# Output projections: the second weight slab split into two halves that TensorE awaits one by one, with ScalarE's table load moved behind the third slab

## The reference

```python
for i in range(DEPTH):                      # DEPTH = 4
    a = rms_norm(h, mix_norm_pre[i])
    m = (dilated_attention_mixer, short_conv_mixer, conformer_conv_mixer)[i % 3](a, ...)
    h = h + rms_norm(m, mix_norm_post[i])
    f = conv_ffn(rms_norm(h, ffn_norm_pre[i]), ffn_w_in[i], ffn_w_conv[i], ffn_w_out[i])
    h = h + rms_norm(f, ffn_norm_post[i])
```

## Time and profile before

| | |
|---|---|
| time of three runs | 2284.12 us median (2284.03 to 2288.83) |
| the profiled execution | 2280.8 us, span 2278.9 us |
| granted TensorE clock, mean | 0.983 |
| TensorE busy | 2190.1 us, 96% |
| weight loads of TensorE busy | 2004.7 us, 88% |
| VectorE busy | 1516.2 us, 67% |
| ScalarE busy | 1010.2 us, 44% |
| GpSimd busy | 461.5 us, 20% |
| chain of work that ended last | TensorE 85%, VectorE 9%, ScalarE 4% |

### The profile page before, as it was taken

One profiled execution on the slowest core, in us unless ns is written; L12 is line 12 of the kernel. 1 busy time (PEld: TensorE's weight loads), 2 busy tenths in 40 slices (PEclk: granted clock), 3 DMA queues, 4 the chain that ended last, 5 costly groups with the idle time before them and its releaser, 6 DMA issues.

```text
span 2278.9 us, 43583 instructions
## 1 busy us (share of the span) xinstructions
PE 2190.1 (96%) x16355; PEld 2004.7 (88%) x16355; DVE 1516.2 (67%) x2436; ACT 1010.2 (44%) x1355; POOL 461.5 (20%) x492
## 2 busy tenths in 40 slices
PE   6999999999999989999999999999999999989999
PEld 5998779978899868699889987799789999869999
DVE  6874868847688577388578848688465545645553
ACT  4334555534455433455443345555353342444342
POOL 2220005500145140035212200055013200100330
PEclk9999999999999989999999999999999999899999
DMA  5555135555545543245555551355545556103554
GB/s 170 184 184 184 38 127 175 185 192 165 192 163 185 178 130 121 69 162 184 180 167 187 185 190 41 109 177 184 190 153 166 175 175 189 43 1 130 184 187 145
DMA packets 299894, 350.28 MB, mean 154 GB/s; under 512 B 7494, under 2 KB 254940, under 8 KB 299804
## 3 DMA queue, kind: packets, MB, share of 16 engines
q1 hardware_dynamic: 298082, 347.07, 46.0%
q10 hardware_dynamic: 1466, 1.80, 0.2%
q0 software_dynamic: 256, 0.17, 0.0%
HBM read 346.34 MB, written 2.68 MB: 153 GB/s over the span
## 4 chain that ended last, share of the span: by engine, by line
PE 85%; DVE 9%; ACT 4%; issue 1%; DMA 1%; SPq 0%; ACTq 0%; DVEq 0%
PE ps L1980 25%; PE ps L1982 25%; PE ps L1981 24%; DVE w_lo L1461 3%; ACT w_hi L1092 2%; PE ps L2310 2%; PE ps L2281 1%; PE ps L2257 1%; DVE res L1583 1%; PE ps L2268 1%; DVE scaled_out L1577 1%; DVE a_lo L1487 1%; PE ps L930 1%; PE ps L2251 1%; DVE hstat L1520 1%
## 5 line engine op out<-in xcount | busy, mean ns | idle before, releaser
L1461 DVE TENSOR_TENSOR w_lo<-raw,w_hi 128x2048 fp32r<-128x2048 f32 (+2 forms) x328 | 744.4, 2270 | 534.4 <-ACT w_hi L1092 534.4
L1980 PE MATMUL ps<-a_hi,w_hi 128*128 128x256 f32 (+1 forms) x3352 | 953.5, 284 | 15.5 <-DVE a_lo L1487 7.6
L1981 PE MATMUL ps<-a_lo,w_hi 128*128 128x256 f32 (+1 forms) x3352 | 948.3, 283 | 0.0
L1982 PE MATMUL ps<-a_hi,w_lo 128*128 128x256 f32 (+1 forms) x3352 | 948.1, 283 | 0.0
L1092 ACT CAST w_hi<-raw 128x2048 fp32r<-128x2048 f32 (+2 forms) x328 | 613.4, 1871 | 626.7 <-PE ps L1982 603.7
L1980 PEld LDWEIGHTS ps<-a_hi,w_hi 128*128 128x128 f32 x3352 | 635.4, 190 | 20.3 <-DVE w_lo L1461 14.4
L1982 PEld LDWEIGHTS ps<-a_hi,w_lo 128*128 128x128 f32 x3352 | 635.8, 190 | 0.0
L1981 PEld LDWEIGHTS ps<-a_lo,w_hi 128*128 128x128 f32 x3352 | 632.7, 189 | 0.1
L1908 POOL TENSOR_TENSOR hs<-sg,cv 128x256 f32<-128x256 f32 x88 | 65.4, 743 | 734.4 <-DVE cv L1745 734.4
L1915 POOL CAST hid_hi<-hs 128x256 f32 (+3 forms) x132 | 140.2, 1062 | 329.1 <-DVE hs L1791 314.9
L1980 PE MATMUL ps<-w_hi,hid_hi 128*128 128x512 f32 x480 | 190.4, 397 | 10.7 <-DVE w_lo L1461 10.4
(11 more groups left out here) (277 smaller groups left out, 2462.0 us busy)
## 6 DMA issues: line engine op xcount, KB each, us to landing
raw<-in_ffn_w_in_dram SPq DMA_DIRECT2D x88, 1024.0 KB, 5.0
raw<-in_attn_w_qkv_dram SPq DMA_DIRECT2D x72, 1024.0 KB, 4.9
raw<-in_ffn_w_out_dram SPq DMA_DIRECT2D x32, 1024.0 KB, 5.0
raw<-in_ffn_w_gate_dram SPq DMA_DIRECT2D x22, 1024.0 KB, 5.1
raw<-in_ffn_w_up_dram SPq DMA_DIRECT2D x22, 1024.0 KB, 5.2
raw<-in_ffn_w_down_dram SPq DMA_DIRECT2D x16, 896.0 KB, 4.7
raw<-in_ffn_w_out_dram SPq DMA_DIRECT2D x16, 768.0 KB, 4.2
raw<-in_sc_w_in_dram SPq DMA_DIRECT2D x12, 1024.0 KB, 5.1
```

The source lines that it names most:

```text
L1461: dve.tensor_tensor(slab_view(w_lo, ph, j, j % 2), slab_view(raw, ph, j, j % 2), slab_view(w_hi, ph, j, j % 2).bitcast(F32), ALU.subtract) ...
L1980: pe.matmul(o, wh, xh, start=start, stop=False)
L1981: pe.matmul(o, wh, xl, start=False, stop=False)
L1982: return pe.matmul(o, wl, xh, start=False, stop=stop)
```

## The change

In an `out` phase the split of slab 1 is cut into two halves of two k tiles each (1024 values per partition instead of 2048). ScalarE raises `hi_half` after the first half and `hi_ready` after the second; VectorE does the same with `lo_half` and `lo_ready`. TensorE waits for `lo_half` before the first matmul of slab 1 and for `lo_ready` before its third k tile of the first token half. The table load of Sqrt moves from ahead of slab 1 to behind the cast of slab 2. Both new semaphores are raised once in a phase, and the wait's value is the count of output projections so far (`B["post"] + 1`).

```diff
--- before.py
+++ after.py
@@ -421,6 +421,7 @@
 
         raw_landed = [sem(f"raw_landed{j}") for j in range(2)]
         hi_ready, lo_ready, mid_used = sem("hi_ready"), sem("lo_ready"), sem("mid_used")
+        hi_half, lo_half = sem("hi_half"), sem("lo_half")
         tile_done, drained_a, drained_b = sem("tile_done"), sem("drained_a"), sem("drained_b")
         x_landed, ident_landed, const_landed = sem("x_landed"), sem("ident_landed"), sem("const_landed")
         hot_landed = sem("hot_landed")
@@ -1089,7 +1090,11 @@
 
                 act.wait_ge(raw_landed[j % 2], (i * (ph.spb // 2) + (ph.s0 // 2 + j // 2 + 1)) * 16)
                 slot_free(act, ph, i, j)
-                act.copy(slab_view(w_hi, ph, j, j % 2), slab_view(raw, ph, j, j % 2)).then_inc(hi_ready, 1)
+                o, src = slab_view(w_hi, ph, j, j % 2), slab_view(raw, ph, j, j % 2)
+                if ph.kind == "out" and j == 1:
+                    act.copy(o[:, 0:2, :], src[:, 0:2, :]).then_inc(hi_half, 1)
+                    o, src = o[:, 2:, :], src[:, 2:, :]
+                act.copy(o, src).then_inc(hi_ready, 1)
 
             def split_ahead(ph, i, is_last):
                 if not is_last:
@@ -1212,7 +1217,6 @@
 
                 elif ph.kind == "out":
                     q0 = 4 * B["post"]
-                    load_table(act, ACT.Sqrt)
 
                     def square(n):
                         act.wait_ge(tile_done, B["t"] + n + 1)
@@ -1233,6 +1237,8 @@
 
                     for j in range(1, ph.spb):
                         split_hi(ph, 0, j)
+                        if j == 2:
+                            load_table(act, ACT.Sqrt)
                     split_ahead(ph, 0, True)
                     square(0)
                     bias_of_root(0, 1)
@@ -1457,9 +1463,14 @@
 
             def split_lo(ph, i, j):
 
+                o, src, hi = slab_view(w_lo, ph, j, j % 2), slab_view(raw, ph, j, j % 2), slab_view(w_hi, ph, j, j % 2)
+                if ph.kind == "out" and j == 1:
+                    dve.wait_ge(hi_half, ph.base["post"] + 1)
+                    dve.tensor_tensor(o[:, 0:2, :], src[:, 0:2, :], hi[:, 0:2, :].bitcast(F32), ALU.subtract
+                                      ).then_inc(lo_half, 1)
+                    o, src, hi = o[:, 2:, :], src[:, 2:, :], hi[:, 2:, :]
                 dve.wait_ge(hi_ready, i * ph.spb + (ph.s0 + j + 1))
-                dve.tensor_tensor(slab_view(w_lo, ph, j, j % 2), slab_view(raw, ph, j, j % 2),
-                                  slab_view(w_hi, ph, j, j % 2).bitcast(F32), ALU.subtract).then_inc(lo_ready, 1)
+                dve.tensor_tensor(o, src, hi.bitcast(F32), ALU.subtract).then_inc(lo_ready, 1)
 
             def split_ahead(ph, i, is_last):
                 if not is_last:
@@ -2147,12 +2158,17 @@
                     kf = sum(ph.kts[0::2])
                     pe.wait_ge(row_ready, B["tok"])
                     for j in range(ph.spb):
-                        slab_split(ph, 0, j)
+                        if j == 1:
+                            pe.wait_ge(lo_half, B["post"] + 1)
+                        else:
+                            slab_split(ph, 0, j)
                         k0 = sum(ph.kts[j % 2:j:2])
                         wh, wl = wide_view(w_hi[j % 2], ph.kts[j]), wide_view(w_lo[j % 2], ph.kts[j])
                         for t in range(2):
                             n, c = 2 * (j % 2) + t, slice(t * P, (t + 1) * P)
                             for k in range(ph.kts[j]):
+                                if j == 1 and t == 0 and k == 2:
+                                    slab_split(ph, 0, 1)
                                 if j % 2 == 0 and t == 0:
                                     pe.wait_ge(hid_ready, B["hid"] - kf + k0 + k + 1)
                                 mm = mm3(out_chunk(n), hid_hi[:, k0 + k, c], hid_lo[:, k0 + k, c], wh[:, k, :], wl[:, k, :],
```

## The result

The changed kernel takes 2272.0 us in the median of six runs (2267.12 to 2278.49), the kernel before 2287.3 in the median of its six (2284.03 to 2288.83). The ratio is 0.9942 with a 95% interval of 0.9925 to 0.9959, which is 13.3 us of 2287 (9 to 17). The forecast was 2269.3 us in a range of 2263.5 to 2276.0 and a gain of 14.8 us. The profiled execution of the changed kernel took 2267.12 us, span 2265.3 against 2278.9. The ratios leave out one slow execution, 3340.8 us long at a mean clock of 0.596, of the kernel with the conformer's slab 1 split early.

A forecast was written before the change was run, and what follows sets the result against it. TensorE was taken to wait for `w_lo` between slabs 0 and 1 of eight output projections. Attentions 1.3, feed-forwards 6.8, short convolution 0.7 and conformer 6.0 make 14.8 us: 2284.1 becomes 2269.3 us, range 2263.5 to 2276.

The forecast's parts named there:

- The waits and their costs: Border of slabs 0 and 1, eight projections: attention costs 0.65 us each, feed-forward 1.70, short convolution about 0.7, conformer 6.63.
- The table load: ScalarE reaches slab 1's cast 1.40 us sooner in seven projections; behind slab 2's cast the load costs nothing.
- The halves: In slab 1's split, half casts take 1.05 us and half subtractions 1.2; the first half alone decides.
- the halves do nothing: Rival, slab 1's split: the table load does all, 8.4 us gained in sum, 2275.7 us; chance 0.06.
- The conformer: Conformer projection's slab border: the pause's cost falls from 3.89 to 0.6 us and the clock's 2.74 go, 6.0 gained.
- the clock's part: Conformer's slab 1 at half clock after the pause: 2.74 us, all to be gained; rival that it isn't, chance 0.10.
- What was late next: Slabs 2 and 3: no new gap; closest case the conformer's slab 3, ready at 955.1 against a need at 955.6.
- The slower rival: Rival, norm pauses behind projections: the clock falls there instead, 4.9 us slower, 2289 us; chance 0.02.
- The base of the forecast: Median of three runs of the kernel before, 2284.1 us, from which the forecast gain was subtracted.

The follow-up runs named there:

- more halves: The changed kernel with slab 1 also split in halves in the phases that follow a norm: 2265.3 us, ratio 0.9917.
- and the conformer's slab 1 early: The kernel with more halves, its conformer's slab 1 also split during the convolution in front of the projection: ratio 0.9918.

## Why the prediction was right

**The waits and their costs.** Each gap cost what the distances of slabs said and not what the idle column said. With 0.34 us of idle time an attention projection gained 0.61 and 0.67, with 1.43 a feed-forward one gained 1.70. That step carried 8.8 us of the sum, and the kernel without the conformer's part measured 8.7 by stages and 8.2 (5.5 to 10.7) by timing.

**The table load.** Hidden behind slab 2's cast as forecast, with 2.11 us of ScalarE's idle time left at the feed-forward.

**The halves.** A half cast was right at 1.05 us. A half subtraction was right at 1.2 us at attention, short convolution and conformer, and too low at the feed-forward by up to 0.5, where GpSimd shares the time. The forecast had named 0.3 for that. The slack of TensorE covered it. In the changed kernel the halves matter least: with the load moved, the whole slab is in time without them in six projections. Only at the short convolution (0.6 us) and at the conformer do they shorten a pause. The rival "the halves do nothing" came near this but was wrong by size: it expected 8.4 where the table load alone gave 12.3 by stages. 1.0 of the difference is at the feed-forward ones, where it had a subtraction of 2.58 us that takes 2.29 at its new time; 2.9 are at the conformer, 4.3 against its 1.4, since it left slab 1 at half the clock, and slab 1 took 5.67 us there.

**The conformer.** The term that was mis-sized: 6.0 forecast, 5.26 in the first profile, 6.15 in the second, both from the one profile of before that the forecast knew. Its 17.82 us were the longest of three (17.82, 16.52, 17.69); from mean to mean the gain is 5.2. The pause's 3.3 us were had in both. Of the clock's 2.74 us, all were had in the second; in the first a slow stretch lay in slab 0 and made it 1.4 us longer, which covered the small pause, so the two slabs took 0.9 more than in the second. Of the seven profiles in which this stage was changed in whole or in part, five have slow matmuls in slab 0 (7.0 to 7.8 us to slab 1, the longest with 0.55 of idle time in it) and two have none (6.01 and 6.02). Of the six in which slab 1 comes as before, two have them. I had taken the slow matmuls for an effect of the pause behind slab 0 alone. So the 2.74 forecast as the clock's part came in full only in the execution whose slab 0 stayed at full clock. TensorE is also quiet ahead of slab 0, when it waits for the normalised values: from 934 to 936 us in the changed kernel's first profile it was busy for 0.93 of 2.00 us, and the clock is at 1.2 GHz right behind, with the share 0.50:

```profile
934.00:936.00 2.00, 0.93 (x5) 0.43 (x5) 0.85 (x2) 1.91 (x6) 0.00 (x0) 1.00 0.00 0
936.00:938.00 2.00, 1.50 (x6) 1.20 (x7) 0.85 (x2) 1.94 (x5) 0.00 (x0) 0.70 0.00 0
938.00:940.00 2.00, 2.00 (x6) 1.52 (x6) 0.92 (x3) 1.94 (x6) 0.00 (x0) 0.50 0.00 0
```

In the second profile TensorE was about as quiet at this place and the clock stayed up:

```profile
934.00:936.00 2.00, 1.01 (x7) 0.60 (x8) 0.85 (x2) 1.94 (x6) 0.00 (x0) 1.00 0.00 0
936.00:938.00 2.00, 2.00 (x11) 1.65 (x10) 0.99 (x3) 1.94 (x6) 0.00 (x0) 1.00 0.00 0
```

So that the quiet ahead of slab 0 brings the slow clock is argued from the order of the rows, and it doesn't do so each time.

The Trainium skill's statement that the number of slow matmuls varies between runs of one kernel ("TensorE: Matmul & The Clock Gate", section "What's actually happening") is borne out: slab 0 of the changed kernel's conformer began slow in one profile and at full clock in the other.

**What was late next.** Nothing, as computed: slabs 2 and 3 follow at 5.53 to 5.54 us in all eight projections, the load of slab 3 at the conformer included, issued at 944.18 in the changed kernel against 947.85.

**The slower rival.** The clock fell behind the same three projections in both first profiles and no oftener. The stretch behind the first attention, in the changed kernel, answering to the earlier trace rows:

```profile
320.00:332.00 12.00, 11.05 (x61) 9.65 (x60) 10.13 (x25) 6.67 (x14) 0.00 (x0) 0.72 0.38 138
```

In the second profile of the changed kernel it fell behind one more, the last feed-forward projection:

```profile
1649.00:1651.00 2.00, 2.00 (x6) 0.87 (x7) 1.93 (x4) 0.00 (x0) 0.00 (x0) 0.50 0.77 263
```

A fall behind that projection is in five of the six profiles of kernels that have both the halves and the moved load, and in one of the seven others. In the four stretches of 2 us from 1647 to 1655 the share was 0.94, 0.50, 0.71 and 1.00, so this one cost at most 1.7 us (an estimate: 8 us less the same at these shares). The rival's mechanism may thus be real at a small size; these few profiles don't prove it, and the timing contains it.

**The time.** 14.8 forecast, 14.0 by stages, 13.6 by the two first spans, 13.3 (9 to 17) by the timing. Each span divides into the eight stages of two slabs, the stretches ahead of and between them, and what follows slab 1 of the last projection, the second stack above all (first three rows: the kernel before; last two: the changed kernel with more):

| profile | eight stages, us | ahead and between | behind |
|---|---|---|---|
| before, first | 104.5 | 1502.9 | 671.5 |
| before, second | 103.2 | 1506.2 | 676.9 |
| before, third | 104.4 | 1506.1 | 673.8 |
| changed, first | 90.4 | 1506.5 | 668.4 |
| changed, second | 89.6 | 1505.5 | 678.3 |
| more halves | 89.5 | 1502.9 | 670.1 |
| and the conformer's slab 1 early | 90.5 | 1502.0 | 676.0 |

In the stretches that the change does not touch, the two first profiles differ by +3.6 us between the stages and by -3.1 behind them. The other profiles show both to be spread: between the stages the first profile of before was the low one, with the other two at the 1506 us of the changed kernel, and behind them one kernel varies by 10 us. The stages alone moved with the change, by 14.0 us from mean to mean. That the forecast's 14.8 and the timing's 13.3 are so near is partly luck, since the timing's own interval is 4 us wide on either side.

The base of the forecast, 2284.1, was low: the median of before became 2287.3 with three further runs, and 2285.3 over the 51 runs timed with the experiments. The 2269.3 lay 2.7 below the measured 2272.0: the base accounts for 1.2 of it by those 51 runs, the gain for the 1.5 by which 14.8 is above 13.3.

## What to carry to other kernels

Cost a wait at a pipeline's border by the distance between equal instructions on either side of it, not by the idle column, which left out 0.3 us of each gap here. When two cures shorten the same hidden piece of work, price each against the slack of the cover: here either alone gave 12 us by stages and both gave 14. After such a change look for the same wait in the neighbouring phases; halving the slab behind each norm was worth another 3 to 4 us by the profiles (5.7 by a loose timing). And look at the longest wait that is left behind the program's start: behind the second feed-forward projection TensorE stands idle for 7.26 us, longer than at any of the eight borders, while VectorE adds to the residual beside GpSimd's long operations. In the kernel before:

```profile
818.73 6.52 DVE L1583 TENSOR_TENSOR res<-res,scaled_out 128x512 f32<-128x512 f32 x2
...
825.30 0.69 PE L2010 MATMUL ps<-ident,res 128*128 128x128 f32 x2 [7.26 <-DVE res L1583]
```

Two such additions take 1.28 us where GpSimd is idle (at 319.85). No run here tried to move GpSimd's work.

## What the runs showed of the hardware that was not expected

- VectorE and GpSimd beside each other: one subtraction of VectorE of 2048 columns took 2.29 us and stretched GpSimd's cast from 0.40 to 2.51; two of 1024 columns took 3.0 to 3.4 us together in the same place, and GpSimd's operations were stretched to 1.27 and 1.59. It goes the other way too: a subtraction that began 0.46 us after a long operation of GpSimd had begun took 5.25 us (819.03 and 818.57, above). The rows fit one account: whichever of the two begins first goes on, and the other stands until it has ended; the border between VectorE's halves let GpSimd in. That this is the mechanism is argued from these rows, not tested by itself.
- The spread of the runs is mostly the clock's: over the 51 timed runs of the kernel before, time and mean granted clock (0.979 to 0.986) correlate at -0.82, and 0.001 of clock goes with 1.5 us. Much of it lies in the second stack's attention, whose mean clock over 110 us was 0.80, 0.86 or 0.91 in executions of code that is the same there. A part that is not the clock's is the pause behind the second feed-forward projection, 7.3 to 12.4 us long.
